# Attention stage of a hybrid decoder layer: output blocks five slots behind their tile, the first tile's gates waited for apart

## What is computed

```python
u = rmsnorm(x, g_pre); P = u @ w_in
# group B, 4 heads x 128, for each query over the keys that the indexer selected
s = q @ k.T * 128**-0.5                 # -inf where not selected
b = softmax(s) @ v * silu(P['sa_z'])
# group C, 4 heads x 128, over 256 memory tokens
c = softmax(q_m @ mem_k.T * 128**-0.5) @ mem_v * silu(P['mem_z'])
y = x + rmsnorm(concat(a, b, c) @ w_out, g_post)
```

## Time and profile before

| | us |
|---|---|
| median of 3 runs | 2798.51 (2794.93 to 2802.18) |
| the profiled execution | 2797.95 |
| its span | 2796.1 |
| TensorE busy | 2711.5 (97%) |
| VectorE, ScalarE, POOL busy | 1247.9, 581.9, 409.7 |
| block products of this stage (line 2231), in the chain that ended last | 7% of the span |

### The profile page before, as it was taken

The page is one execution under the profiler, slowest core; times in us unless marked ns, Lnnn a source line. Parts: engine busy times, 40 slices in busy tenths (PEclk is TensorE's granted clock), DMA queues, the critical chain, the costliest instruction groups (busy, mean ns, idle before and its releaser), DMA issues.

```text
span 2796.1 us, 35927 instructions
## 1 busy us (share of the span) xinstructions
PE 2711.5 (97%) x13915; PEld 1928.1 (69%) x13915; DVE 1247.9 (45%) x2149; ACT 581.9 (21%) x1369; POOL 409.7 (15%) x826
## 2 busy tenths in 40 slices
PE   7998999999999999999999999999689999899998
PEld 6674468856844588888888888888555565455553
DVE  3242588867854663142222144452132232345553
ACT  3122458760000000000000100101132222122211
POOL 0000014320000000000000022320113200333341
PEclk9999999999999999999999999999889999999999
DMA  6457312212222221222341354552654411975652
GB/s 230 104 154 253 105 39 69 82 36 73 84 79 89 83 64 54 73 68 88 107 130 61 106 155 140 151 182 94 228 190 137 134 50 41 295 238 167 210 168 85
DMA packets 272694, 342.00 MB, mean 122 GB/s; under 512 B 40876, under 2 KB 225444, under 8 KB 267244
## 3 DMA queue, kind: packets, MB, share of 16 engines
q1 hardware_dynamic: 238924, 262.19, 30.1%
q0 software_dynamic: 16528, 67.92, 8.0%
q10 hardware_dynamic: 17072, 9.58, 1.1%
HBM read 262.16 MB, written 80.01 MB: 122 GB/s over the span
## 4 chain that ended last, share of the span: by engine, by line
PE 85%; DMA 2%; SPq 2%; DVE 1%; issue 1%; ACT 0%; POOL 0%; DVEq 0%; ACTq 0%
PE sbank L1486 44%; PE sbank L1483 10%; PE kept_bank L3274 8%; PE kept_bank L2231 7%; PE sbank L1366 2%; PE at_bank_dots L2213 1%; PE kept_bank L2257 1%; PE mo_bank_dots_num L3239 1%; PE mo_bank_kv L3250 1%; PE sbank L1329 1%; PE sbank L1251 1%; PE mo_bank_kv L3297 1%; PE at_bank_turn L2201 1%; DMA area<-proj 1%; DMA attention_then_units<-gate_rows 1%
## 5 line engine op out<-in xcount | busy, mean ns | idle before, releaser
L1486 PE MATMUL sbank<-w,xT 128*128 128x256 f32 x3200 | 699.8, 379 | 0.0
L1486 PEld LDWEIGHTS sbank<-w,xT 128*128 128x128 f32 x3200 | 605.9, 190 | 85.0 <-issue 3.3
L1486 PE MATMUL sbank<-w,area 128*128 128x256 f32 x1664 | 361.4, 379 | 0.0
L1966 DVE TENSOR_TENSOR pout_b<-pout_b,sbank 128x256 f32<-128x256 f32 x320 | 134.3, 421 | 498.9 <-PE sbank L1486 410.2
L1486 PEld LDWEIGHTS sbank<-w,area 128*128 128x128 f32 x1664 | 315.8, 190 | 42.8
L1929 DVE TENSOR_TENSOR w<-w 128x2048 f32<-128x2048 f32 x63 | 142.8, 2289 | 318.9 <-PE sbank L1486 255.7
L1581 ACT ACTIVATE pout_b<-sbank 128x256 f32<-128x256 f32 x120 | 45.2, 383 | 890.5 <-PE sbank L1486 658.3
L1486 PE MATMUL sbank<-w 128*128 128x256 f32 x832 | 181.9, 379 | 2.6 <-issue 2.6
L1486 PEld LDWEIGHTS sbank<-w 128*128 128x128 f32 x832 | 157.9, 190 | 24.2 <-issue 2.8
L1483 PE MATMUL sbank<-xT,w 128*128 128x512 f32 x384 | 166.6, 593 | 0.0
L1483 PEld LDWEIGHTS sbank<-xT,w 128*128 128x128 f32 x384 | 72.7, 190 | 90.1 <-issue 90.0
(11 more groups left out here) (478 smaller groups left out, 3457.8 us busy)
## 6 DMA issues: line engine op xcount, KB each, us to landing
w<-in_w_in SPq DMA_DIRECT2D x64, 1024.0 KB, 5.3
proj<-pout_b SPq DMA_DIRECT2D x208, 128.0 KB, 1.7
area<-in_x_prompt SPq DMA_DIRECT2D x16, 1024.0 KB, 7.4
attention_then_units<-proj SPq DMA_DIRECT2D x128, 128.0 KB, 3.1
area<-roped_q_of_decode POOLq DMA_DIRECT2D x32, 256.0 KB, 4.1
w<-in_w_out SPq DMA_DIRECT2D x4, 2048.0 KB, 17.7
y_of_groups_b_c<-out_parts SPq DMA_DIRECT2D x32, 256.0 KB, 2.2
mo_dec_states<-in_state_mlstm_C SPq DMA_DIRECT2D x32, 256.0 KB, 5.6
```

Of the source, the lines that this page charges most:

```text
L1486: last = nc.tensor.matmul(bank[t][:, 0:256], x(c, t * P, (t + 1) * P), at[name][:, c, :], start=first_ and c == 0, stop=c == 7, skip_group ...
L1966: nc.vector.tensor_tensor(out[:, t, :], x[:, t, :], product_at(n, t), ALU.add).then_inc(sums_read, 1)
```

## The change

- `A_LAG` goes from 6 to 5: block n is computed in slot n + 5.
- Both halves of a block stand behind `mix`: the first directly behind it, the second where it was.
- The loads of z count on a semaphore of their own, `z_in`; `dots` and `logits` wait for three transfers in place of five, and `finish_m` of a tile's first head waits for z.
- POOL's gathers wait for the first tile's three transfers.
- `memory_out` and the clearing of `p_spread` stand ahead of VectorE's slots.
- SP's store of the last block is left out of the loop (the block behind it does it), and ahead of handing over to the next stage SP also waits for all heads in `hT`.

```diff
@@ -1983,7 +1983,7 @@
 O_W = 512
 O_B = D // O_W
 A_UNITS = QT * H
-A_LAG = 6
+A_LAG = 5
 
 
 BC_OWN = A_UNITS - O_B
@@ -2008,7 +2008,7 @@
         S("dec_out"), S("dec_out_stored"), S("dec_out_loaded"), S("dec_z_loaded"), S("dec_out_gated"))
     od_turned, (od_kept,) = S("dec_out_turned"), k.queue_sems("dec_out_kept", 1)
 
-    loaded = k.sems("tile_loaded", 2)
+    loaded, z_in = k.sems("tile_loaded", 2), k.sems("tile_z_loaded", 2)
     w_in, y_out = k.queue_sems("w_bc_loaded", O_B), k.queue_sems("y_part_stored", 2)
     k.y_part_out, (k.attention_over,) = y_out, k.queue_sems("attention_over", 1)
     dotted, read, max_ready, p_ready = S("sa_dots"), S("sa_dots_read"), S("sa_max"), S("sa_p")
@@ -2089,7 +2089,7 @@
                     sp.dma_start(v, outs["prompt_v"].rearrange("(c p) n -> p c n", p=P)).then_inc(v_keys_in, 16)
                     sp.dma_start(mv[:, :, :], outs["prompt_mem_v"].rearrange("(c p) n -> p c n", p=P)).then_inc(mv_in, 16)
                 for j, c in enumerate((C_SZ, C_MZ)):
-                    sp.dma_start(z[:, u, j, :], k.proj[rows, c:c + HW]).then_inc(loaded[u], 16)
+                    sp.dma_start(z[:, u, j, :], k.proj[rows, c:c + HW]).then_inc(z_in[u], 16)
 
             load(0)
             sp.wait_ge(k.last_out, 64)
@@ -2110,7 +2110,7 @@
                     sp.wait_ge(m_finished, H * (t - 1))
                     load(t)
                 n = group(s - 1)
-                if n is not None:
+                if n is not None and n < BC_OWN - 1:
                     sp.wait_ge(evacuated, n + 1)
                     sp.dma_start(k.y_part[n // O_B * P:(n // O_B + 1) * P, n % O_B * O_W:(n % O_B + 1) * O_W],
                                  out[:, n % 2, :]).then_inc(y_out[n % 2], 16)
@@ -2152,6 +2152,7 @@
             pool.wait_ge(k.last_out, 64)
             for t in range(DEC_T):
                 nc.gpsimd.dma_start(kn[:, t, :], k.kn4[t].rearrange("b t (h d) -> (b t h) d", h=H)).then_inc(small_in, 16)
+            pool.wait_ge(loaded[0], 48)
             for q in range(QUADS):
                 j, c = q // 2, q % 2
                 if q >= 2:
@@ -2204,7 +2205,7 @@
             def dots(s):
                 t, h = s // H, s % H
                 if h == 0:
-                    pe.wait_ge(loaded[t % 2], 80 * (t // 2 + 1))
+                    pe.wait_ge(loaded[t % 2], 48 * (t // 2 + 1))
                 if s:
                     pe.wait_ge(read, s)
                     pe.wait_ge(m_kept, s)
@@ -2295,12 +2296,12 @@
                     turn_p(s - 1)
                 if s < A_UNITS:
                     dots(s)
-                if group(s) is not None:
-                    multiply(group(s), 0)
                 if 2 <= s <= A_UNITS + 1:
                     turn_h(s - 2)
                 if 1 <= s <= A_UNITS:
                     mix(s - 1)
+                if group(s) is not None:
+                    multiply(group(s), 0)
                 if s == 3:
                     turn_logits()
                 if s == 5:
@@ -2455,7 +2456,6 @@
             def memory_out():
                 dve.wait_ge(closed, 1)
                 nc.vector.tensor_copy(oc[:], acc[:, 0:DH]).then_inc(out_ready, 1)
-                nc.vector.memset(spread[:], 0.0).then_inc(masks, 1)
 
             def own_head(dst, src):
 
@@ -2480,7 +2480,7 @@
                 t, u, wd = s // H, s % 2, width(s)
                 dve.wait_ge(dotted, s + 1)
                 if s % H == 0:
-                    dve.wait_ge(loaded[t % 2], 80 * (t // 2 + 1))
+                    dve.wait_ge(loaded[t % 2], 48 * (t // 2 + 1))
                 if s:
                     dve.wait_ge(p_ready, s)
                 for b in range((wd + 511) // 512):
@@ -2504,6 +2504,8 @@
 
             def finish_m(s):
                 t, h, u = s // H, s % H, s % 2
+                if h == 0:
+                    dve.wait_ge(z_in[t % 2], 32 * (t // 2 + 1))
                 dve.wait_ge(m_ready, s + 1)
                 order.step(nc.vector.reciprocal(mrr[:, u:u + 1], mrs[:, u:u + 1]))
                 dve.wait_ge(m_mixed, s + 1)
@@ -2513,6 +2515,8 @@
                                                z[:, t % 2, 1, h * DH:(h + 1) * DH], ALU.mult, ALU.mult
                                                ).then_inc(m_finished, 1)
 
+            nc.vector.memset(spread[:], 0.0).then_inc(masks, 1)
+            memory_out()
             for s in slots:
                 if 1 <= s <= A_UNITS:
                     keep(s - 1)
@@ -2523,8 +2527,6 @@
                     finish(s - 1)
                 if s < A_UNITS:
                     finish_m(s)
-                if s == 0:
-                    memory_out()
                 if s == 2:
                     decode_logits()
                 if s == 3:
@@ -2550,6 +2552,7 @@
         def _(sp):
             n = BC_OWN - 1
             sp.wait_ge(evacuated, n + 1)
+            sp.wait_ge(h_kept, A_UNITS)
             k.clear(sp)
             sp.sem_inc(k.attention_over, 1)
             sp.dma_start(k.y_part[n // O_B * P:(n // O_B + 1) * P, n % O_B * O_W:(n % O_B + 1) * O_W],
```

## The result

The changed kernel takes 2819.57 us (median of 4 runs, 2816.26 to 2821.57) against 2798.05 us for the kernel before on the same chip: a ratio of 1.0073, 95% interval 1.0061 to 1.0085, so 21.5 us more. Slower was the likeliest sign in the prediction, but the time lies above its 2807.6 and also above the end of its range, 2817. The profiled execution took 2817.89 us, 19.94 more than the one before.

What follows compares the result with a forecast made beforehand. TensorE was taken to bound slots 6 to 33, a chain of engines those before. Terms -8.0 + 0 + 0.5 + 15.5 + 1.7 - 0.6 = +9.1 us; 2797.95 + 9.1 + 0.56 = 2807.6 us, range 2799 to 2817.

Steps and rivals of the forecast that it cites:

- Slower: Whole kernel: slower by over 0.3% was given chance 0.52, within 0.41, faster 0.07.
- Part 1, z: Start of the stage: first dots stop waiting for z, so slot 1's maxima come 8.0 us earlier, bounds 6.5 and 10.
- Part 2, slots 5 and 33: Products one slot earlier: slot 33 loses 7.08 us, slot 5 grows by 7.1, net 0; plus 0.5 for slot 5's clock.
- Part 3, the stalls: Slots 9, 13 to 29: TensorE waits for keep_h behind the exponentials, six stalls, 15.5 us lost, bounds 13.1 and 17.9.
- Part 3, the clock: Behind the six stalls: TensorE's clock falls once, 1.7 us lost, bounds 0 and 10.2.
- Rival B: Slots 9 to 29: the clock falls at every stall, +17.6 us, so 2816; chance 0.13.
- rival C: Stalls without a clock fall, and z gains 10 us, not 8: +5.4, so 2804; chance 0.25.
- Part 4, order: Other slots: both halves behind the mix change no sum, costed at 0, with 0.5 us on either side.
- Part 4, end: Handover to the next stage: its loads start earlier before the last product's end, gain 0.6 us, bounds 0 and 1.
- A: The forecast itself, six stalls and one clock fall: 2807.6 us, own range 2804 to 2811; chance 0.50.
- D: Slots 9 to 29: no stall, as ScalarE reaches keep_h before TensorE reaches the product: 2790 to 2788; chance 0.07.
- E: An unseen wait, such as gathers or stores meeting earlier slots, adds over 10 us: 2818 and more; chance 0.05.

Runs made afterwards that it cites:

- e7: The kernel before with the first tile's part alone (distance six, old order), and the gathers held until z has landed: 2789.61 us, 0.9959.
- e12: Changed kernel; in slots with a tile's first block keep_h ahead of the exponentials, elsewhere the first half back in its old place; gathers wait for z: 2794.08 us, 0.9975.
- e8: Changed kernel without the first tile's part (z back on the shared semaphore, gathers not held, clearing in slot 0): 2825.81 us, 1.0087.
- e11: The changed kernel, unaltered, run once more for a second profile: 2812.38 us in one run.
- e6: Changed kernel with three useless matmuls ahead of the wait for the head in slots 9, 13 to 29: 2812.48 us, 1.0040.
- e2: Changed kernel with the distance back at six, both halves still behind the mix: 2795.14 us, 0.9985.
- e4: Changed kernel with keep_h issued by ScalarE ahead of weigh_m and weigh, not behind them: 2793.59 us, 0.9978.
- e3: Changed kernel with the first half back ahead of turn_h and mix, save in slots with a tile's first block: 2819.74 us, 1.0074.
- e9: The kernel before, unaltered, run once more for a second profile: 2803.3 us in one run.
- e1: The kernel before with the first tile's part of the change alone; distance six and the old order of halves stay: 2792.24 us, 0.9970.
- e10: The kernel before with the first tile's part alone, run once more for a second profile: 2793.75 us in one run.

## Why the prediction was off

The stalls were foreseen in place, cause and size. Two terms of the sum were mis-sized, and both lie between slot 6 and the next stage: the clock's falls, taken as 1.7 us and 5.1 in the profile (6.0 as a mean of four), and the new order in the other slots, taken as nothing and 3.2 us.

**Part 1, z: right.** Forecast -8.0 us at the maxima of slot 1, measured -7.8; the first dots at 2003.19 (forecast 2003.6), the mix of slot 0 at 2016.89 (2017), the maxima at 2019.61 (2019.5). One guess in it was wrong without harm: the 0.6 us that the held gathers were to give z. z came at 2018.85 and before at 2018.96. e7 and e12 show that the mechanism is real, 4.5 us, but wants the gathers held until z is down.

**Part 2, slots 5 and 33: right, but for 0.2 us and a bound.** Slot 5 is 12.72 us long; the forecast was 12.2, and 0.5 for the clock. Slot 33 lost 6.9 us and not 7.08, since the last head's transposes stay in it, from 2391.92 to the next stage at 2392.23:

```profile
2391.92 0.38 PE L2244 MATMUL at_bank_turn<-ident_sb,at_ho 128*128 128x128 f32 x2
```

In e8 and e11 slot 5 took 14.24 and 14.34 us at clocks of 0.82 and 0.81 (after: 0.90), 2.0 and 2.1 us over 12.2, so the upper bound of its clock term, 1.7, was too low.

**Part 3, the stalls: right in place, cause and size.** The slots without a fall (of after, e6, e8 and e11) grow by 2.29, 2.44, 2.64, 2.79, 2.94 and 3.08 us: 16.2, forecast 15.5, bounds 13.1 and 17.9. e2 and e4 each take them away, the second without touching the distance.

**Part 3, the clock: the step that failed most.** "Stalls of 2.2 to 3.0 us lie between the two rows, nearer to the one without a fall. ... I take one fall". There were three in the profile, and in the four profiles with such stalls (after, e3, e8, e11) 3, 3, 4 and 4 of 6: 14 of 24. The same stall in e11, with no fall behind it (5.40 us in the kernel after):

```profile
2291.14 3.70 PE L2232 MATMUL kept_bank<-w,hT_of_odd_tiles 128*128 128x512 f32 x8 [2.68 <-ACT hT_of_odd_tiles L2374]
```

The price of one, 1.7 us, was right. So the term is 14/24 x 6 x 1.7 = 6.0 us on average where 1.7 was taken. Slot 17 fell 4 times of 4, slot 9, with the shortest stall, once; but slots 21 and 25, longer than 17, only twice each, so length alone does not decide. One row on either side of an unknown length was no reason to go with the nearer; between a certain fall and none, the middle of the bounds (5.1) would have been closer. Rival B had the other extreme; its 2816, with the 3.2 us of Part 4, is close to what came, but by luck: it had six falls where there were three.

The Trainium skill, "TensorE: Matmul & The Clock Gate", section "Why this matters for your kernels", warns only of idle gaps longer than any of these. The stalls here are 2.0 to 2.8 us by the brackets, and the clock fell behind more than half of them; by that rule there would have been no fall, as in rival C, so here the measurement decides against it. The Trainium skill, the same page, Part 1, "What's actually happening", says that the moment of a transition varies from run to run of one kernel, and with that the profiles agree: the same stall in slot 25 has a fall in after and e8 and none in e3 and e11.

**Part 4, order: a term costed at nothing, the other step that failed.** "What they hid still is" looked at what the mix waits for and not at `turn_h`, which waits for VectorE's copy and which the first half also covered; and it counted on dots behind the transposes, which slot 32 doesn't have. Slots 24 and 32 cost 2.00 and 1.22 us. The work that makes VectorE late there, the decode's last steps in slot 24, stood in the trace of before, hidden under the half.

**Part 4, end: nothing to see.** The next stage's first load is issued at 2385.69, 16.78 us later than before while the last product ends 17.2 us later: 0.4 us gained at the handover, forecast 0.6. In the first pair of profiles the stretch behind is 2.3 us longer, in the second 2.3 us shorter; it does not carry the difference on.

**The sum again.** From slot 6 to the next stage the forecast was 15.5 + 1.7 - 7.1 = +10.1 us, measured +17.7: 0.7 of stalls, 3.4 for two more falls, 3.2 for slots 24 and 32, 0.2 in slot 33 and 0.1 in the rest. That is 7.6 of the 10.8 us that the profile's +19.94 lies over the forecast's +9.1. The other 3.2 are the next stage (+2.3, where -0.6 was forecast) and 0.3 in the remaining pieces; e9 and e11 show that as variation between executions. Between the profiles' +19.94 and the medians' +21.5 lie 1.6 us that no row explains, and that the spread of the runs (5 us) covers.

**The rivals.** A had the right mechanism, B the clock, in part. C (no fall) and D (no stall) did not happen; e4 is what D asked for, `keep_h` ahead of `weigh`, and it gave 2793.59 where D had 2788 to 2790; the 3.2 us of slots 24 and 32 are about the difference. E's unseen wait exists, at 3.2 us and not over 10.

## What to carry to other kernels

How close a consumer can follow in a software pipeline is set by the queue of the engine that hands over, not by the data alone: look for what is issued ahead of the handing-over instruction in the same slot, and move that instruction before shortening the distance. When a filler is moved, list every wait that it stood ahead of, not only the one it is moved for. And an idle time in a stretch where TensorE runs at the full clock costs its own length and, perhaps, a stretch at half the clock, so a range for it must reach to a fall behind every one; transfers that are not needed yet belong behind the one that the path waits for.

## What the runs showed of the hardware

- Idle times of 2.0 to 2.8 us between dense fp32 products were followed by a fall to 1.2 GHz in 14 of 24 cases, each worth 1.7 us; with useless products in the same gaps there was none in 6 (e6), and the kernel was 7 us faster by the medians for doing more.
- The profiled executions of kernels that are equal up to there began the stage anywhere from 1992.16 to 2001.55 us, which alone moves a span by up to 9 us. Cutting an execution at marks and comparing the pieces (321.29, 321.28, 321.28 and 321.29 us for the same slots in before, e9, e1 and e10) tells tenths of a microsecond where whole times tell some 3 us.
- Eight gathers issued on POOL ahead of z's landing (from 2003.3 on in the kernel after) delayed that load of SP, issued before them, by some 5 us: in the kernels with z on its own semaphore VectorE waited for it until 20.1 to 20.8 us after the bias was issued (nine profiles), and until 15.2 and 15.1 us in e7 and e12, which hold the gathers back.
